# A hybrid block on one core: the memory's second value unit moves from the banded attention to the first norm

## The chip, the cores and the metric

The kernel runs on one core of a Trainium2 chip. The metric is the device time of one execution in microseconds (us), lower is better. The core has five engines with queues of their own that meet only at semaphores: TensorE (PE) for matmuls, VectorE (DVE), ScalarE (ACT), GpSimd (POOL) and SyncE (SP), which only issues DMAs here.

## What is computed

Two blocks in a row over 256 tokens of width 1024, in float32. The change lies in the first block:

```python
def first_block(x, mem, ...):
    h = hybrid_mixer(x, w_in, ...)            # mLSTM and banded attention, then @ w_out
    x = layer_norm(ALPHA * x + h, ln1_g, ln1_b)
    h = memory_cross_attention(x, mem, xa_wq, xa_wkv, xa_wo)
    x = layer_norm(ALPHA * x + h, ln2_g, ln2_b)
    ...

def memory_cross_attention(x, mem, wq, wkv, wo):
    q = (x @ wq).reshape(B, S, XA_HEADS, XA_HEAD_DIM)
    k, v = jnp.split(mem @ wkv, 2, axis=-1)
    ...
```

`mem` is an input of 256 rows of width 1024 and doesn't depend on `x`. So `mem @ wkv`, 1024 columns of keys and 1024 of values, can be multiplied at any time before the cross attention reads it.

## The kernel before

**Products.** A float32 product is made of three matmuls of rounded halves (`three`): high times high, low times high and high times low. Each operand has a high half in the rounded type and a low half, the rest. `hir` and `lor` hold the halves of the weights, `INH`/`INL` those of an activation, `HIH`/`HIL` those of another (here of `mem` in tiles 0 to 7 and of the mixer's output `mix` in tiles 8 to 15).

**Units and chunks.** A unit is 256 columns of a weight, in chunks of four 128-row tiles (48 matmuls of 256 columns), or, for values, a wide unit of 512 columns, in chunks of two tiles (48 matmuls of 512 columns, `wide_g`). The keys of the memory are the units kv 0 to 3, the values the wide units kv 4 and kv 5. The function `weight_plan` lists all chunks in order of use, and between them 48 rows "mod" of the modulation weights of the second block, which VectorE alone multiplies with a vector. A chunk costs a DMA of 512 KB into one of six raw buffers (SP waits until the chunk six places earlier has been split), an ACT instruction that rounds it (`hir<-raw`), and a DVE instruction that subtracts (`lor<-raw,hir`).

**Staging ahead.** The class `Ahead` decides where these two instructions stand in the queues of ACT and DVE. `take` is called where a unit's chunk comes due. It issues the split of that chunk if need be, then of the next ones until three are ahead. There are four slots for split chunks, so a chunk can be split only when the matmuls of the chunk four places earlier are done.

**The attention.** The mLSTM and the banded attention (`swa`, groups 0 and 1) are generators, and `rotate` interleaves their steps with those of a filler, `projections`, in the code of each engine. The filler runs through the first projections, then kv 0 to 5. A step of a wide unit's filler is one chunk, 12 matmuls. In `swa`, TensorE multiplies logits, ACT and DVE make probabilities, TensorE transposes these (12 per group), ACT copies the results out, and TensorE multiplies with the values (`ps<-FA` 128x512). DVE copies both groups' output, and ACT and DVE split it into tiles 4 to 7 of `mix`. What is left of the filler runs after the last product, ahead of the output projection, units wout 0 to 3.

**The first norm.** Behind each wout unit, DVE adds it to `X` and ACT squares `X`. The norm sums over features with one-column matmuls (`row_sums`: what is early, then the last part of `X`, then its squares), DVE and ACT make the mean and the factor of each token, TensorE broadcasts both over the partitions (`spread_bank`), and DVE subtracts and multiplies tile by tile (UNITS: one tile, one, then pairs). ACT scales them to `INH`, and for the pairs a second time to `X`, and DVE subtracts the low half `INL`. Then the query units xq 0 and xq 1 run interleaved over the eight tiles, with four chunks of weights, and xq 2 and xq 3 behind them.

Names: in the rows, L1595 and L1598 are helpers of DVE, L1096 the rounding of weights on ACT, L1226 and L1176 the copies of transposed probabilities and of values, L754 the transposes, L1259 and L1264 the two scalings of the norm.

Of the kernel before, what the change touches and what calls it, by code (L numbers as in the profile page):

```python
# [132 lines left out]
def weight_plan(A):  # L133

    plan = []
# [52 lines left out]
    for c in range(2):  # L188
        add_wide(("kv", 4 + c), A["xa_wkv"], 1024 + 512 * c, 8, mod=2)
    for c in range(4):  # L190
# [5 lines left out]
        add_mod(int(c < 3))  # L196
    add2(("xq", 0), A["xa_wq"], 0, ("xq", 1), A["xa_wq"], 256, mod=1)
# [124 lines left out]
def build(nc, A, out):  # L322
    with ExitStack() as ctx:
# [182 lines left out]
        def tensor(e):  # L506
# [58 lines left out]
            def wide_g(key, kt, x, pool=lin, apart=0):  # L565
# [19 lines left out]
                for kk in range(both):  # L585
                    for m in range(2):
                        step(kk, m)
                    if kk % 2 and kk + 1 < kt:
                        yield
# [60 lines left out]
            def projections():  # L650
# [14 lines left out]
                for c in range(2):  # L665
                    yield from wide_g(("kv", 4 + c), 8, mem)
                    yield
# [103 lines left out]
            def row_sums(name, c, src):  # L771
# [6 lines left out]
                t.then_inc(*mm.up((name, "early")))  # L778
                w.wait_ge(dve.at((name, "x", 3)))
                for m in range(2):  # L780
                    for i in range(2):
                        column(b[:, m:m + 1], src[:, i, :], m, o1024, last=i == 1)
                w.wait_ge(act.at((name, "sq", 3)))
# [10 lines left out]
            def layer_norm(name):  # L794
                row_sums(name, 3, X[:, 6:8, :])
                spread_bank((name, "mu"), SN[:, 0:2])
                spread_bank((name, "r"), SN[:, 6:8])
# [4 lines left out]
            layer_norm("n1")  # L802
# [273 lines left out]
        def scalar(e):  # L1076
# [72 lines left out]
            def projections():  # L1149
# [22 lines left out]
                for c in range(2):  # L1172
                    yield from ahead.unit_g(("kv", 4 + c), 8, 2)
                    for m in range(2):
                        w.wait_ge(mm.at(("unit", ("kv", 4 + c), m)))
                        e.activation(VC[:, m, 512 * c:512 * c + 512], bank["unit", ("kv", 4 + c), m], ACT.Copy).then_inc(  # L1176
                            *act.up(("out", ("unit", ("kv", 4 + c), m)), *(["KV"] if c and m else [])))
                    yield
# [71 lines left out]
            def layer_norm(name, gn, bn, inp, free):  # L1250
                if ahead.next < len(plan) and plan[ahead.next][3] is True and ahead.room():
# [3 lines left out]
                for k, n in UNITS:  # L1255
                    d = X[:, k:k + n, :]
# [1317 lines left out]
```

## Time and profile before

| | |
|---|---|
| median of 3 runs | 906.94 us (902.21, 906.94, 906.99) |
| the profiled execution | 907.06 us |
| its span on the core | 905.3 us |
| PE busy | 860.5 us, 95% |
| DVE busy | 651.4 us, 72% |
| ACT busy | 503.7 us, 56% |
| 16 DMA engines, queue of the weights | 57.0% |
| granted clock of TensorE, mean | 0.97 |

In the profile, times count from the start of the span, and a row of the timeline can stand for several instructions in a row (x12), with the idle time of the engine ahead of them and what ended it in brackets. A float32 matmul of attention or norm appears as more than one record. A matmul's duration runs over the next one's start, so the pitch between starts tells its cost. PEclk is the granted clock of TensorE: 1.00 is 2.4 GHz, 0.50 is 1.2 GHz.

### The profile page before, as it was taken

Reading aid. Unit: us, or ns where it says so; the run is one execution under the profiler, and the core shown is the slowest. Engines: PE = TensorE matmul, PEld = TensorE weight load, DVE = VectorE, ACT = ScalarE, POOL = GpSimd, SP = SyncE. Lnnn points to the kernel's source line nnn. Section 1 sums busy time; section 2 is a strip of 40 time slices with the busy share of each in tenths; the row PEclk is TensorE's granted clock in tenths of the full one; section 3 lists DMA queues with packets and bytes.
Section 4 is the critical chain, followed back from the end, with each engine's and each line's share of the span. In section 5 each row is a group of like instructions: output and inputs, shape, how many; then the busy total and the mean of one; then the engine's idle time right before and its main releaser. Section 6 shows DMA issues by size and latency. Waiting matters only on the chain.

```text
span 905.3 us, 15843 instructions
## 1 busy us (share of the span) xinstructions
PE 860.5 (95%) x6396; PEld 810.8 (90%) x6396; DVE 651.4 (72%) x1011; ACT 503.7 (56%) x723; POOL 7.6 (1%) x17
## 2 busy tenths in 40 slices
PE   8899997999899999999997999999899899999997
PEld 7789986889799999999997899898899899999886
DVE  5765787678567988887867896787798766665553
ACT  5643447455447666655455756777657554444342
POOL 0200000000000000000000000000000000000000
PEclk9999999989998999999998999999999799999999
DMA  9974556756062665667862376455575177775751
GB/s 339 244 216 138 171 182 195 215 172 229 28 185 72 214 186 185 187 196 240 261 210 70 118 251 185 147 187 181 169 233 166 60 250 225 233 233 186 168 204 47
DMA packets 139592, 166.89 MB, mean 184 GB/s; under 512 B 5520, under 2 KB 123280, under 8 KB 139520
## 3 DMA queue, kind: packets, MB, share of 16 engines
q1 hardware_dynamic: 137712, 162.82, 57.0%
q0 software_dynamic: 720, 2.02, 1.2%
q8 instruction: 50, 0.82, 0.4%
q10 hardware_dynamic: 1088, 1.05, 0.3%
q14 instruction: 22, 0.18, 0.1%
HBM read 164.62 MB, written 1.25 MB: 183 GB/s over the span
## 4 chain that ended last, share of the span: by engine, by line
PE 32%; DVE 12%; ACT 8%; issue 3%; DVEq 0%; ACTq 0%
PE ps L512 32%; DVE lor L1595 5%; DVE FA L1595 3%; ACT hir L1096 2%; DVE FA L1598 1%; ACT L1434 1%; DVE INL L1595 0%; ACT X L1366 0%; DVE raw L1612 0%; ACT HIH L1372 0%; ACT FA L1434 0%; DVE FA L2256 0%; DVE FA L1601 0%; ACT FA L1476 0%; DVE X L1595 0%
## 5 line engine op out<-in xcount | busy, mean ns | idle before, releaser
L1595 DVE TENSOR_TENSOR lor<-raw,hir 128x1024 fp32r<-128x1024 f32 (+1 forms) x267 | 309.9, 1178 | 118.8 <-ACT hir L1096 112.6
L1096 ACT ACTIVATE hir<-raw 128x1024 fp32r<-128x1024 f32 (+1 forms) x257 | 260.2, 1032 | 125.1 <-PE ps L512 105.3
L512 PE MATMUL ps<-INH,hir 128*128 128x256 f32 (+1 forms) x1064 | 306.9, 288 | 4.2 <-ACT INH L1259 2.5
L512 PE MATMUL ps<-INH,lor 128*128 128x256 f32 (+1 forms) x1064 | 302.4, 284 | 2.8 <-DVE lor L1595 2.7
L512 PE MATMUL ps<-INL,hir 128*128 128x256 f32 (+1 forms) x1064 | 303.0, 285 | 1.4 <-DVE INL L1595 1.2
L512 PEld LDWEIGHTS ps<-INH,hir 128*128 128x128 f32 x1064 | 204.9, 193 | 7.4 <-issue 6.1
L512 PEld LDWEIGHTS ps<-INH,lor 128*128 128x128 f32 x1064 | 204.5, 192 | 4.9 <-DVE lor L1595 3.9
L512 PEld LDWEIGHTS ps<-INL,hir 128*128 128x128 f32 x1064 | 204.0, 192 | 2.4 <-DVE INL L1595 2.4
L512 PE MATMUL ps<-HIH,lor 128*128 128x256 f32 x688 | 195.5, 284 | 5.2 <-DVE lor L1595 5.2
L512 PE MATMUL ps<-HIH,hir 128*128 128x256 f32 x688 | 197.9, 288 | 0.0
L512 PE MATMUL ps<-HIL,hir 128*128 128x256 f32 x688 | 194.0, 282 | 0.0
L512 PEld LDWEIGHTS ps<-HIH,lor 128*128 128x128 f32 x688 | 130.6, 190 | 7.5 <-DVE lor L1595 6.6
L512 PEld LDWEIGHTS ps<-HIH,hir 128*128 128x128 f32 x688 | 130.8, 190 | 4.1 <-issue 3.2
L512 PEld LDWEIGHTS ps<-HIL,hir 128*128 128x128 f32 x688 | 131.1, 191 | 0.0
L1598 DVE SCALAR_TENSOR_TENSOR FA<-ps,vec,FA 128x254 f32<-128x254 f32 (+2 forms) x130 | 53.2, 474 | 17.8 <-ACT FA L1106 17.8
L512 PE MATMUL ps<-hir,HIH 128*128 128x512 f32 (+1 forms) x136 | 54.0, 397 | 8.9 <-DVE HIL L1595 6.1
L1612 DVE SCALAR_TENSOR_TENSOR raw<-raw,cb 128x1024 f32<-128x1024 f32 x48 | 58.3, 1219 | 0.7 <-DMA raw<-in_mod_wT 0.7
L512 PE MATMUL ps<-lor,HIH 128*128 128x512 f32 (+1 forms) x136 | 53.0, 390 | 0.0
L512 PE MATMUL ps<-hir,HIL 128*128 128x512 f32 (+1 forms) x136 | 53.0, 390 | 0.0
L1106 ACT ACTIVATE FA<-ps,vec 128x256 f32<-128x256 f32 x58 | 29.4, 558 | 35.4 <-PE ps L512 35.4
L512 PE MATMUL ps<-FA 128*128 128x256 f32 (+6 forms) x212 | 39.8, 372 | 4.3 <-DVE FA L1595 3.5
L512 PEld LDWEIGHTS ps<-hir,HIH 128*128 128x128 f32 x136 | 27.1, 199 | 15.9 <-issue 10.3
(270 smaller groups left out, 793.6 us busy)
## 6 DMA issues: line engine op xcount, KB each, us to landing
raw<-in_w_in SPq DMA_DIRECT2D x64, 512.0 KB, 4.5
raw<-in_mod_wT SPq DMA_DIRECT2D x48, 512.0 KB, 4.5
raw<-in_ffn_w_up SPq DMA_DIRECT2D x44, 512.0 KB, 4.5
raw<-in_w_ffn_in SPq DMA_DIRECT2D x44, 512.0 KB, 4.8
raw<-in_w_ffn_out SPq DMA_DIRECT2D x22, 512.0 KB, 4.4
raw<-in_ffn_w_down SPq DMA_DIRECT2D x20, 512.0 KB, 5.0
raw<-in_xa_wkv SPq DMA_DIRECT2D x16, 512.0 KB, 3.8
raw<-in_xa_wq SPq DMA_DIRECT2D x8, 512.0 KB, 5.7
```

Of the source, the lines that this page charges most:

```text
L512: return e.matmul(o, l, r, start=start, stop=stop, skip_group_check=True)
L1096: e.activation(hi, src, ACT.Copy).then_inc(*w_hi.up(i))
L1106: e.activation(o[:, b, :], p[:, b * T:(b + 1) * T], ACT.Identity, scale=V(wname, (K - 1) * nb + i + b), bias=V(bname, i + b)).then_inc(*ac ...
L1434: e.activation(dst, wide2(bank["unit", ("gl", c)]), ACT.Sigmoid).then_inc(*act.up(("out", ("unit", ("gl", c)))))
L1595: return e.tensor_tensor(o, a, b, op)
L1598: return e.scalar_tensor_tensor(out=o, in0=a, scalar=s, in1=b, op0=op0, op1=op1)
L1612: e.scalar_tensor_tensor(out=v, in0=v, scalar=1.0, in1=CB[:, :], op0=MUL, op1=MUL, accum_out=MOD[:, key[1]:key[1] + 1]).then_inc(*dve.up(key))
```

## The change

The plan of weights lists kv 5 behind the wout units instead of behind kv 4, and its two mod rows now stand behind kv 4, four in all. `projections` ends with kv 4 on all three engines. TensorE multiplies kv 5 in steps of three matmuls (`fine`) between the steps of the first norm, and what is left, ahead of the queries, with banks of the attention's pool. In the norm's code of ACT and DVE, `next(other)` takes the chunks of kv 5, and so stages the queries' chunks. The copy of the values (`values(1)`) stands behind the norm.

```diff
 weight_plan:
-    for c in range(2):
-        add_wide(("kv", 4 + c), A["xa_wkv"], 1024 + 512 * c, 8, mod=2)
+    add_wide(("kv", 4), A["xa_wkv"], 1024, 8, mod=4)
...
+    add_wide(("kv", 5), A["xa_wkv"], 1536, 8)
     add2(("xq", 0), A["xa_wq"], 0, ("xq", 1), A["xa_wq"], 256, mod=1)
 tensor, wide_g:
-            def wide_g(key, kt, x, pool=lin, apart=0):
+            def wide_g(key, kt, x, pool=lin, apart=0, fine=False):
...
                     for m in range(2):
                         step(kk, m)
-                    if kk % 2 and kk + 1 < kt:
+                        if fine:
+                            yield
+                    if kk % 2 and kk + 1 < kt and not fine:
                         yield
 tensor, row_sums and layer_norm:
                 t.then_inc(*mm.up((name, "early")))
+                fill(2)
                 w.wait_ge(dve.at((name, "x", 3)))
...
+                fill(1)
                 w.wait_ge(act.at((name, "sq", 3)))
...
+                row_sums(name, 3, X[:, 6:8, :], fill)
+                fill(1)
                 spread_bank((name, "mu"), SN[:, 0:2])
+                fill(2)
                 spread_bank((name, "r"), SN[:, 6:8])
...
-            layer_norm("n1")
+            values = wide_g(("kv", 5), 8, mem, att, fine=True)
+            layer_norm("n1", lambda n: steps_of(values, n))
+            run(values)
 scalar (vector alike, without the values):
-            def layer_norm(name, gn, bn, inp, free):
-                if ahead.next < len(plan) and plan[ahead.next][3] is True and ahead.room():
+            def layer_norm(name, gn, bn, inp, free, other=None):
+                if other:
+                    next(other)
+                elif ahead.next < len(plan) and plan[ahead.next][3] is True and ahead.room():
                     ahead.stage()
...
                 for k, n in UNITS:
+                    if other and k in (0, 2, 4):
+                        next(other, None)
...
-            layer_norm("n1", "ln1_g", "ln1_b", x1, "x1 free")
+            layer_norm("n1", "ln1_g", "ln1_b", x1, "x1 free", ahead.unit_g(("kv", 5), 8, 2))
+            values(1)
```

**DVE at the end of the attention.** The rows from the last chunks of kv 4 to the probabilities of both groups (`small` holds their sums, `raw,cb` is a mod row). Before:

```order
L1595 TENSOR_TENSOR lor<-raw,hir 128x1024 x2
L1612 SCALAR_TENSOR_TENSOR raw,small<-raw,cb 128x1024 x2
L1595 TENSOR_TENSOR lor<-raw,hir 128x1024
L1595 TENSOR_TENSOR small<-small 128x8
L1796 RECIPROCAL small<-small 128x8
L1601 TENSOR_SCALAR FA<-FA,small 128x128 x4
```

After:

```order
L1609 TENSOR_TENSOR lor<-raw,hir 128x1024 x2
L1626 SCALAR_TENSOR_TENSOR raw,small<-raw,cb 128x1024 x4
L1609 TENSOR_TENSOR lor<-raw,hir 128x1024
L1609 TENSOR_TENSOR small<-small 128x8
L1809 RECIPROCAL small<-small 128x8
L1615 TENSOR_SCALAR FA<-FA,small 128x128 x4
```

Four mod rows now stand ahead of the first group's probabilities where two stood; the split behind them is that of a wout chunk.

**PE in the first norm.** From the sums of the last `X` (`con,X`) and its squares (`con,SQ`) to the broadcasts (`con,small`). Before, with the first query matmuls (`INH`) behind them:

```order
L512 MATMUL ps<-con,X 128x1 x4
L512 MATMUL ps<-con,SQ 128x1 x4
L512 MATMUL ps<-con,small 128x128 x4
L512 MATMUL ps<-INH,hir 128x256
L512 MATMUL ps<-INH,lor 128x256
L512 MATMUL ps<-INL,hir 128x256
```

After:

```order
L512 MATMUL ps<-con,X 128x1 x4
L512 MATMUL ps<-hir,HIH 128x512
L512 MATMUL ps<-hir,HIL 128x512
L512 MATMUL ps<-lor,HIH 128x512
L512 MATMUL ps<-con,SQ 128x1 x4
L512 MATMUL ps<-hir,HIH 128x512
L512 MATMUL ps<-hir,HIL 128x512
L512 MATMUL ps<-lor,HIH 128x512
L512 MATMUL ps<-con,small 128x128 x2
```

Three matmuls of kv 5 stand in each gap here, six ahead of the first row and six between the two broadcasts, and 30 behind the second, ahead of the queries.

**ACT in the first norm.** From the root (`small`) through the scalings to `INH` and `X` to the next roundings of weights (`hir`). Before:

```order
L1254 ACTIVATE small<-small 128x2
L1259 ACTIVATE INH<-X,vec 128x256 x4
L1264 ACTIVATE X<-X,vec 128x256 x2
L1259 ACTIVATE INH<-X,vec 128x256 x2
L1264 ACTIVATE X<-X,vec 128x256 x2
L1259 ACTIVATE INH<-X,vec 128x256 x2
L1264 ACTIVATE X<-X,vec 128x256 x2
L1096 ACTIVATE hir<-raw 128x1024 x7
```

After:

```order
L1265 ACTIVATE small<-small 128x2
L1103 ACTIVATE hir<-raw 128x1024
L1272 ACTIVATE INH<-X,vec 128x256 x2
L1103 ACTIVATE hir<-raw 128x1024
L1272 ACTIVATE INH<-X,vec 128x256 x2
L1277 ACTIVATE X<-X,vec 128x256 x2
L1103 ACTIVATE hir<-raw 128x1024
L1272 ACTIVATE INH<-X,vec 128x256 x2
L1277 ACTIVATE X<-X,vec 128x256 x2
L1272 ACTIVATE INH<-X,vec 128x256 x2
L1277 ACTIVATE X<-X,vec 128x256 x2
L1186 ACTIVATE FA<-ps 128x512 x2
```

The three roundings between the scalings are those of the first three query chunks; each is for a slot that kv 5 must free. The fourth comes behind the copies of the last row. DVE's splits stand in the same places.

## Rows read from the trace of the kernel before

**Rows 1.** the page: busy us of an engine (share of the span) xinstructions

```profile
PE 860.5 (95%) x6396; PEld 810.8 (90%) x6396; DVE 651.4 (72%) x1011; ACT 503.7 (56%) x723; POOL 7.6 (1%) x17
```

**Rows 2.** timeline, PE, end of the attention (start us, us, engine line op tiles)

```profile
150.08 2.47 PE L754 MATMUL ps<-con,FA 128*128 128x128 f32 x12 [2.59 <-DVE FA L1601]
...
152.20 0.78 PE L512 MATMUL ps<-hir,HIH 128*128 128x512 f32 x1
...
155.86 1.47 PE L754 MATMUL ps<-con,FA 128*128 128x128 f32 x12
157.08 0.48 PE L512 MATMUL ps<-hir,HIH 128*128 128x512 f32 x1
...
160.03 3.71 PE L512 MATMUL ps<-FA 128*64 128x512 f32 x12
163.67 0.49 PE L512 MATMUL ps<-hir,HIH 128*128 128x512 f32 x1
...
169.09 0.40 PE L512 MATMUL ps<-lor,HIH 128*128 128x512 f32 x1
```

**Rows 3.** timeline of DVE at the end of the attention

```profile
144.24 1.22 DVE L1612 SCALAR_TENSOR_TENSOR raw<-raw,cb 128x1024 f32<-128x1024 f32 x1
...
146.53 1.22 DVE L1595 TENSOR_TENSOR lor<-raw,hir 128x1024 fp32r<-128x1024 f32 x1
...
148.10 1.93 DVE L1601 TENSOR_SCALAR FA<-FA,small 128x128 f32<-128x128 f32 x8
...
151.51 1.93 DVE L1601 TENSOR_SCALAR FA<-FA,small 128x128 f32<-128x128 f32 x8
...
166.19 1.23 DVE L1595 TENSOR_TENSOR HIL<-FA,HIH 128x1024 fp32r<-128x1024 f32 x1 [1.13 <-ACT HIH L1101]
```

**Rows 4.** timeline of PE in and behind the first norm; the last: cross attention

```profile
193.50 1.05 PE L512 MATMUL ps<-con,X 128*128 128x1 f32 x8 [0.51 <-DVE X L1598]
...
196.11 2.25 PE L512 MATMUL ps<-con,small 128*128 128x128 f32 x8 [0.25 <-DVE small L1853]
199.60 0.55 PE L512 MATMUL ps<-INH,hir 128*128 128x256 f32 x1 [1.24 <-ACT INH L1259]
...
205.22 0.28 PE L512 MATMUL ps<-INH,hir 128*128 128x256 f32 x1
...
211.94 0.28 PE L512 MATMUL ps<-INH,hir 128*128 128x256 f32 x1
...
229.83 0.66 PE L825 MATMUL ps<-con,FA 128*128 128x128 f32 x4 [1.17 <-DVE FA L1601]
```

**Rows 5.** three stretches of PE: length, busy us (x), PEclk, DMA share, GB/s

```profile
150.00:153.80 3.80, 3.72 (x16) 0.56 0.78 282
153.80:160.00 6.20, 6.20 (x34) 0.99 0.84 249
196.00:205.00 9.00, 7.57 (x31) 0.50 0.03 10
```

**Rows 6.** timeline of ACT at the end of the attention

```profile
144.94 2.94 ACT L1096 ACTIVATE hir<-raw 128x1024 fp32r<-128x1024 f32 x3
147.79 1.06 ACT L1176 ACTIVATE FA<-ps 128x512 f32<-128x512 f32 x2
```

**Rows 7.** timeline of SP's queue, end of the attention: weight requests

```profile
140.90 3.87 SPq L2443 DMA_DIRECT2D raw<-in_xa_wkv  x2
```

**Rows 8.** timeline of DVE in the first norm

```profile
195.89 0.16 DVE L1853 COPY small<-ps 128x4 f32<-128x4 f32 x1 [2.45 <-PE ps L512]
...
198.40 1.21 DVE L1595 TENSOR_TENSOR X<-X,ps 128x256 f32<-128x256 f32 x3 [0.61 <-PE ps L512]
...
204.68 1.22 DVE L1595 TENSOR_TENSOR lor<-raw,hir 128x1024 fp32r<-128x1024 f32 x1
205.81 1.40 DVE L1595 TENSOR_TENSOR X<-X,ps 128x512 f32<-128x512 f32 x2
```

**Rows 9.** timeline of ACT in the first norm

```profile
202.88 1.09 ACT L1264 ACTIVATE X<-X,vec 128x256 f32<-128x256 f32 x2
```

More of the change, by code:

```diff
@@ L664, in projections @@
                     yield
-                for c in range(2):
-                    yield from wide_g(("kv", 4 + c), 8, mem)
-                    yield
+                yield from wide_g(("kv", 4), 8, mem)
+                yield
             b, before = att.get("uf", bank)
@@ L769, in tensor, with row_sums @@
             run(fill)
-            def row_sums(name, c, src):
+            def row_sums(name, c, src, fill=lambda n: None):
                 b, before = att.get((name, "sums"), bank)
@@ L792, in spread_bank, with layer_norm @@
                 spread(b, v, name)
-            def layer_norm(name):
-                row_sums(name, 3, X[:, 6:8, :])
+            def layer_norm(name, fill=lambda n: None):
+                row_sums(name, 3, X[:, 6:8, :], fill)
+                fill(1)
                 spread_bank((name, "mu"), SN[:, 0:2])
+                fill(2)
                 spread_bank((name, "r"), SN[:, 6:8])
@@ L1171, in projections, with values @@
                     yield
[L1172 to L1178, printed above, removed]
+                yield from ahead.unit_g(("kv", 4), 8, 2)
+                values(0)
+                yield
+            def values(c):
+                for m in range(2):
+                    w.wait_ge(mm.at(("unit", ("kv", 4 + c), m)))
+                    e.activation(VC[:, m, 512 * c:512 * c + 512], bank["unit", ("kv", 4 + c), m], ACT.Copy).then_inc(
+                        *act.up(("out", ("unit", ("kv", 4 + c), m)), *(["KV"] if c and m else [])))
             w.wait_ge(mm.at("uf f"), dve.at("UC"))
@@ L1712, in projections @@
                     yield
-                for c in range(2):
-                    yield from ahead.unit_g(("kv", 4 + c), 8, 2)
-                    yield
+                yield from ahead.unit_g(("kv", 4), 8, 2)
+                yield
             w.wait_ge(mm.at("uf f"))
@@ L1846, in stats, with layer_norm @@
                     fold(st, (name, "m", 2), (name, "sum"))
-            def layer_norm(name, gn, bn, inp, free):
+            def layer_norm(name, gn, bn, inp, free, other=None):
                 low = None
-                if ahead.next < len(plan) and plan[ahead.next][3] is True and ahead.room():
+                if other:
+                    next(other)
+                elif ahead.next < len(plan) and plan[ahead.next][3] is True and ahead.room():
                     low = ahead.enter()
@@ L1877, in layer_norm @@
                 for k, n in UNITS:
+                    if other and k in (0, 2, 4):
+                        next(other, None)
                     d = X[:, k:k + n, :]
@@ L1893, in vector @@
                 stats("n1", c, None)
-            layer_norm("n1", "ln1_g", "ln1_b", x1, "x1 free")
+            layer_norm("n1", "ln1_g", "ln1_b", x1, "x1 free", ahead.unit_g(("kv", 5), 8, 2))
             dve.mark("before cross attention")
```

## The prediction, made before the changed kernel ran

> **What bounds the kernel now.** I read the page first: the tensor engine is busy 95% of the span [rows 1]. So a matmul that moves is paid at its new place unless it fills a gap there, and leaves its old place only if the engine has nothing else to wait for. Then I read two stretches in the timelines: the end of the banded attention, from 143 us to the start of the output projection (wout) at 169.3 us, and the first norm, from 192.04 us, the end of wout, to the end of the two interleaved query units.
>
> In the attention the matmuls of the second value unit (key kv 5, called V5 here; 48 wide ones) stand in three pieces: 12 at 152.20 behind the first transposes, 12 at 157.08 behind the second, and 24 from 163.67, behind the last product of probabilities and values [rows 2]. The last piece covers a chain on two other engines: the two attention outputs are copied, rounded and subtracted, until 167.42 [rows 3]. In the norm the engine does little: one-column sums and four broadcasts until 198.36, then it waits until 199.60 for the first normalized tile [rows 4]. That makes some 7.6 us of room for V5, which is 48 x 0.236 = 11.3 us long (the pitch from the first to the last of the 24: 163.67 to 169.09 [rows 2]).
>
> **Part 1: taken out of the attention.** What then ends last is the vector engine. Its next vector multiplies for the modulation (mod) are four in a row now, because the value weights between them are gone: two more at 1.15 us (144.24 to 146.53 for two), ahead of the first probabilities, which began at 148.10. They now end at about 152.3, the second ones (begun at 151.51, 1.9 us long) at 155.7 [rows 3]. Both sets slip by 2.3 us. The transposes of the first follow at 152.4. The engine has then idled for 4.9 us; after 2.6 us of idling the first of the old ones ran at 1.2 GHz (0.56 granted until 153.8), taking 2.1 us where the second, at the full clock, took 1.2 [rows 2, 5]. The second transposes start at 155.8 and, still at 1.2 GHz, end at 157.9; the scalar engine copies the last bank (two such copies took 1.06 us [rows 6]), and the product starts at 158.4. It took 3.64 us at 2.4 GHz (160.03 to 163.67 [rows 2]), and would take 7.3 at half of it. The full clock came back at 153.8, 3.7 us after work resumed [rows 2, 5]; counted from 155.8 that is 159.5 to, allowing for the 5.6 us of the norm (199.60 to 205.22 [rows 4, 5]), 161.4. I take 160.5, so the product ends at 163.0; bounds 162.0 (clock back at once) and 165.5 (never during the product).
>
> The scalar engine is the other guard of that time: it rounds three chunks in a row at 144.94 before its copies [rows 6]. They are now wout chunks. The first takes the place of the first request of the row of 140.90 [rows 7], which had landed by 146.9, when its rounding, the third of those, began. The third is requested at 146.7, when the second mod is done; with the same 5 to 6 us it is rounded by 153, ahead of the first copy. A later landing would push the product out by as much.
>
> Now the cover is gone. Wout begins at 163.0, does 24 matmuls (2.83 us) and then wants the attention's output, low half too, 3.75 us after the product's end (163.67 to 167.42 [rows 2, 3]). It waits 0.7 us. Wout ends at 163.0 + 3.75 + 2.6 + 17.0 = 186.4 instead of 192.04. **Gain 5.6 us**, bounds 3.1 and 6.6. So only half of V5 is won back: its last piece hid a chain, and its first two stood where the vector engine is late anyway.
>
> **Part 2: put into the norm.** I count from the end of wout. On the tensor engine: early sums 0.9 (the eight records of the X sums took 0.9, 193.50, the next ones 0.91 later [rows 4]; the early ones are eight too), 6 matmuls of V5 1.4, the sums of the last X 0.9, 3 matmuls 0.7, the sums of its squares 1.0 (an estimate from the same eight records), at +5.0; 3 matmuls to +5.7; broadcast of the mean, 6 matmuls to +7.6, broadcast of the factor to +8.2 (0.66 with its tail for four records at the full clock, so some 0.5 each [rows 4]). Then 30 matmuls in a row until +15.1. If only this counted, the queries' 96 matmuls at 0.118 (205.22 to 211.94 for 57 [rows 4]) would end at +26.5. Before they ended at 213.7, +21.7. That is a cost of 4.9.
>
> But the weights count too. Before, three of the four first query chunks lay ready ahead of the norm and the fourth was split beside it (204.68 [rows 8]). Now the four slots hold V5, and each query chunk can be rounded only when V5's matmuls have freed a slot, by a scalar and a vector instruction that stand between the norm's steps. The scalar queue: root to +6.0, first chunk to +7.0 (1.0 each [rows 6]). The vector engine waits for that, splits until +8.2 (1.22 [rows 8]), subtracts, and its next multiplication starts at +8.6 instead of at 198.40, +6.4. Pair by pair:
> the second chunk is rounded at +10.3 behind the first two scalings and split until +12.5; tiles 2 and 3 are normalized by +13.8 (1.40 for a pair less the overlap [rows 8]); the scalar engine scales them twice, 1.1 each [rows 9], until +16.0, and only then rounds the third chunk, split at +18.2. Tiles 4 and 5 are normalized at +19.6; the low half of tiles 2 and 3 follows at +20.2. On the scalar engine tiles 4 and 5 last until +21.8 and tiles 6 and 7 until +23.9; then V5's two results are copied (1.05 [rows 6]), and the fourth chunk is rounded until +26.0 and split until +27.2. Nothing covers this last split: it stands behind the whole norm.
>
> The tensor engine follows: V5 ends at +15.1, tiles 0 and 1 are multiplied until +18.0, it waits for the low half of tile 2 until +20.2, works until +23.6, and waits for the fourth chunk until +27.2. The remaining 41 matmuls end at +32.0. **Cost 10.3 us** instead of 4.9. The last wait is 3.6 us long; one of 2.6 us was followed by 1.2 GHz and cost about 1.8 us (transposes 0.9 too long, the 12 wide ones 3.66 instead of 2.8, which is 12 x 0.236 [rows 2, 5]). **Cost 1.8 us**, bounds 0 and 2.3 (24 matmuls at the pitch that they had before 205.22 [rows 4]).
>
> Whether the short pieces in the norm run at 2.4 GHz is not shown in the old norm, which lay at 0.50 from 196 to 205 with one-column work [rows 5]. With 2 matmuls out of 3 us dense between them I take the full clock. The Trainium skill (Perfetto Trace Analysis, Matmul Optimizations) says that power follows utilization and that matmuls should run back to back in batches. That speaks against pieces of 3 and 6; by it the sum would be the third case below, by my reading the first.
>
> Behind the queries nothing changes: the chunks for the third and fourth units are split before the tensor engine gets there (at most four instructions of 1.2 us in the 7 us it still computes), the attention's values are copied 7 us before they are read, and the later stages are bound by the tensor engine, which gives nothing back. The weights' bytes are the same.
>
> **Sum.** -5.6 + 10.3 + 1.8 = **+6.5 us**. The profiled execution took 907.06 us, the median of the runs shown is 906.94; so **913.5 us**. With all bounds: -6.6 + 10.3 + 0 = +3.7 to -3.1 + 10.3 + 2.3 = +9.5.
>
> **Rivals.** First, *the room is real*: the splits don't hold the norm. If the fourth query chunk is split by +21.7, when the tensor engine would want it, and the low halves keep ahead of it, only the 4.9 us remain: -5.6 + 4.9 = -0.7, 906.4 us, and down to 905.3 with the best clock in the attention. For it: the vector engine idled 2.45 us for the sums before [rows 8], and the engine that is 95% busy had a hole there. Against it: the order above, in which the scalar engine reaches the fourth rounding only after the last scaling. The Trainium skill (Perfetto Trace Analysis, Optimization Strategy) recommends interleaving regimes bound by different engines; by it this case would hold. It decides at 5.5 us: by so much must the scalar and vector chain be shorter than my sum. No sum of mine reaches 4.5 us faster.
>
> Second, *the pieces run at 1.2 GHz*. The first gap closes late, V5's pieces cost 0.42 each and free the slots later: 3 + 3 + 6 matmuls at 0.19 more each are 2.3 us, the sums and broadcasts about 1.0 more. The chain above shifts by 3.3 and all behind it: +9.8, 916.9 us.
>
> Third, *the wout weights land late*: the scalar engine waits for the third chunk, two us beyond 153, and the attention ends with it: +8.5, 915.5 us. Against it: the queue is asked for the same bytes per time as before.
>
> **How the numbers follow.** Forecast 0.60; the room is real 0.22; half clock 0.08; late weights 0.05; something faster that I have no price for 0.05. A measurement can tell 0.5%, 4.5 us. Of the forecast's 0.60 some 0.08 falls below 4.5. Slower: 0.52 + 0.13 = 0.65; same: 0.22 + 0.08 = 0.30; faster 0.05. The range takes in the first rival, whose chance is over what may be left out, and the second: 905.0 to 918.0.
>
> **What would show it.** The product of probabilities and values ending near 163, wout's end near 186.4, a wait of about 0.7 us in its first unit. In the norm the vector engine should wait for the scalar engine's roundings (three times), the tensor engine for a low half of tile 2 (2.2 us) and for the fourth query chunk (3.6 us), and the query units should end about 32 us after wout instead of 21.7. If V5 ran into the queries without waits, the first rival holds; if wout ends at 189 or later, part 1 is too hopeful.

## The result, and the profile after

| | before | after |
|---|---|---|
| median | 906.94 us (902.21 to 911.43, 9 runs) | 911.28 us (909.66 to 914.91, 9 runs) |
| the profiled execution | 907.06 us | 912.93 us |
| its span | 905.3 us | 911.1 us |

The ratio after to before is 1.0067, with a 95% interval of 1.0046 to 1.0088: the change costs 6.1 us (4.2 to 8.0) by that ratio. The medians alone differ by 4.3 us, the profiled executions by 5.9 us.

The page of after hides this completely: TensorE does the same work, in nearly the same busy time as in [rows 1].

```profile
PE 859.0 (94%) x6396; PEld 809.2 (89%) x6396; DVE 651.7 (72%) x1011; ACT 503.6 (55%) x723; POOL 7.6 (1%) x17
```

**Where the time went.** ScalarE loads a function table 43 times, always at the same places of the program. Three of these loads bracket the two changed stretches: at the attention's probabilities, at the third wout unit, and at the start of the cross attention. These are the rows of ScalarE's timeline (start us, duration), before and then after:

```profile
128.15 1.28 ACT L1218 ACT_TABLE_LOAD   x1
...
187.93 1.28 ACT L1111 ACT_TABLE_LOAD   x1
...
223.55 1.28 ACT L1284 ACT_TABLE_LOAD   x1
```

```profile
128.28 1.28 ACT L1227 ACT_TABLE_LOAD   x1
...
182.77 1.28 ACT L1118 ACT_TABLE_LOAD   x1
...
229.28 1.28 ACT L1298 ACT_TABLE_LOAD   x1
```

From the first to the second, the attention stage, went from 59.78 to 54.49 us: 5.3 gained. From the second to the third, the norm stage (it has the rest of wout in it, 4.1 us in both), from 35.62 to 46.51 us: 10.9 lost. Every later load comes 5.7 to 5.9 us later than before, up to the last. So in these two executions the whole difference lies in the two stages, and nothing behind them gives back or adds. All experiments below are read with the same two numbers.

**The attention after**, PE's timeline (idle time ahead and what ended it in brackets), against [rows 2]:

```profile
152.50 2.50 PE L755 MATMUL ps<-con,FA 128*128 128x128 f32 x12 [4.88 <-DVE FA L1615]
...
156.93 2.82 PE L755 MATMUL ps<-con,FA 128*128 128x128 f32 x12 [1.92 <-ACT FA L1235]
...
159.68 3.70 PE L512 MATMUL ps<-FA 128*64 128x512 f32 x12
...
167.12 0.38 PE L512 MATMUL ps<-HIL,hir 128*128 128x256 f32 x1 [0.47 <-DVE HIL L1609]
```

With no value matmuls between them, the transposes wait 4.88 us for the four mods, as forecast. The second transposes wait 1.92 us more, and not for VectorE but for ScalarE's copy of the first ones. ScalarE was late since it had stood at a DMA:

```profile
150.15 1.06 ACT L1103 ACTIVATE hir<-raw 128x1024 fp32r<-128x1024 f32 x1 [4.03 <-DMA raw<-in_w_out]
154.36 1.06 ACT L1103 ACTIVATE hir<-raw 128x1024 fp32r<-128x1024 f32 x1 [3.15 <-DMA raw<-in_w_out]
155.32 1.07 ACT L1186 ACTIVATE FA<-ps 128x512 f32<-128x512 f32 x2
```

The third wout chunk is rounded until 155.4, not 153. SP's queue sent its request on time, at 146.77, but it landed 7.6 us later and not 5 to 6. Two rows, SP's timeline and the weights' requests of 138 to 158 us (size, median us to landing):

```profile
146.77 2.41 SPq L2460 DMA_DIRECT2D raw<-in_w_out  x3
```

```profile
raw<-in_w_out SPq DMA_DIRECT2D x3, 512.0 KB, 7.6
```

The clock, in stretches (length, busy us of PE, PEld, DVE, ACT, POOL, then PEclk, DMA share, GB/s):

```profile
149.00:152.00 3.00, 0.00 (x0) 0.00 (x0) 2.93 (x12) 1.06 (x1) 0.00 (x0) 1.00 0.94 296
152.00:154.00 2.00, 1.50 (x9) 1.50 (x10) 1.93 (x6) 0.00 (x0) 0.00 (x0) 0.72 1.14 229
154.00:158.00 4.00, 2.08 (x10) 1.68 (x9) 4.00 (x11) 3.50 (x6) 0.00 (x0) 0.50 1.05 291
158.00:160.00 2.00, 2.00 (x10) 1.54 (x9) 0.13 (x1) 1.41 (x3) 0.00 (x0) 0.57 1.15 202
160.00:163.00 3.00, 3.00 (x12) 0.99 (x10) 0.00 (x0) 0.38 (x1) 0.00 (x0) 1.00 1.03 245
```

The low clock begins within the first transposes (0.72 from 152 to 154), covers the second, and ends ahead of the product of probabilities and values, which took 3.6 us as before. This early end is particular to this execution: in the six others with the same code up to wout (e1, e2, e3, e9, e10, e11 below) the low clock reached into the product, which took 3.9 to 4.3 us.

**The norm after**, PE, against [rows 4]:

```profile
189.15 0.95 PE L512 MATMUL ps<-con,X 128*128 128x1 f32 x8
...
194.16 0.61 PE L512 MATMUL ps<-con,small 128*128 128x128 f32 x4
...
207.47 0.58 PE L512 MATMUL ps<-INL,hir 128*128 128x256 f32 x1 [2.69 <-DVE INL L1609]
...
213.14 0.38 PE L512 MATMUL ps<-INH,hir 128*128 128x256 f32 x1 [0.57 <-ACT hir L1103]
214.50 0.38 PE L512 MATMUL ps<-INH,lor 128*128 128x256 f32 x1 [0.98 <-DVE lor L1609]
```

and the two engines that it waits for, ScalarE and then VectorE, against [rows 9] and [rows 8]:

```profile
200.96 1.09 ACT L1272 ACTIVATE INH<-X,vec 128x256 fp32r<-128x256 f32 x2 [2.71 <-DVE X L1609]
202.09 1.10 ACT L1277 ACTIVATE X<-X,vec 128x256 f32<-128x256 f32 x2
203.09 1.05 ACT L1103 ACTIVATE hir<-raw 128x1024 fp32r<-128x1024 f32 x1
206.85 1.09 ACT L1272 ACTIVATE INH<-X,vec 128x256 fp32r<-128x256 f32 x2 [2.71 <-DVE X L1609]
...
211.08 1.06 ACT L1186 ACTIVATE FA<-ps 128x512 f32<-128x512 f32 x2
212.04 2.94 ACT L1103 ACTIVATE hir<-raw 128x1024 fp32r<-128x1024 f32 x3
```

```profile
198.38 1.23 DVE L1609 TENSOR_TENSOR lor<-raw,hir 128x1024 fp32r<-128x1024 f32 x1 [0.93 <-ACT hir L1103]
...
204.26 1.23 DVE L1609 TENSOR_TENSOR lor<-raw,hir 128x1024 fp32r<-128x1024 f32 x1 [2.56 <-ACT hir L1103]
205.41 1.40 DVE L1609 TENSOR_TENSOR X<-X,ps 128x512 f32<-128x512 f32 x2
206.73 0.68 DVE L1609 TENSOR_TENSOR INL<-X,INH 128x512 fp32r<-128x512 f32 x1
...
213.22 1.23 DVE L1609 TENSOR_TENSOR lor<-raw,hir 128x1024 fp32r<-128x1024 f32 x1 [1.25 <-ACT hir L1103]
```

The reader sees two engines taking turns: VectorE waits 2.56 us for a rounding, ScalarE waits 2.71 us for the tiles that VectorE normalizes behind the split of that rounding, and TensorE waits for what comes out, three times. V5's pieces themselves ran at the full clock (the idle time in the first row is the start of the wait that ends at 207.47), the low one came behind the first wait:

```profile
186.00:206.00 20.00, 18.78 (x115) 16.50 (x113) 12.80 (x23) 8.19 (x13) 0.00 (x0) 1.00 0.41 132
208.00:210.80 2.80, 2.80 (x15) 2.80 (x14) 1.39 (x3) 2.77 (x6) 0.00 (x0) 0.50 0.15 53
```

### The profile page after: what moved, and what is told of

It is laid out like the page before. It is cut to its first block, busy times and chain, and to the rows that moved or that the text cites. A ratio compares the mean times of both kernels' runs of the same rounds, so it can differ in the third digit from the quotient of the medians.

```text
span 911.1 us, 15842 instructions
## 1 busy us (share of the span) xinstructions
PE 859.0 (94%) x6396; PEld 809.2 (89%) x6396; DVE 651.7 (72%) x1011; ACT 503.6 (55%) x723; POOL 7.6 (1%) x17
## 3 DMA queue, kind: packets, MB, share of 16 engines
HBM read 164.62 MB, written 1.25 MB: 182 GB/s over the span
## 4 chain that ended last, share of the span: by engine, by line
PE 30%; DVE 13%; ACT 8%; issue 3%; DMA 1%; DVEq 0%; ACTq 0%; SPq 0%
PE ps L512 30%; DVE lor L1609 5%; DVE FA L1609 3%; ACT hir L1103 2%; DVE FA L1612 1%; ACT L1448 1%; DMA raw<-in_ffn_w_down 1%; DVE INL L1609 0%; ACT X L1380 0%; DVE raw L1626 0%; ACT HIH L1386 0%; ACT FA L1448 0%; DVE FA L2273 0%; DVE FA L1615 0%; ACT FA L1490 0%
## 5 line engine op out<-in xcount | busy, mean ns | idle before, releaser
L1609 DVE TENSOR_TENSOR HIL<-FA,HIH 128x512 fp32r<-128x512 f32 (+2 forms) x34 | 23.4, 690 | 23.6 <-ACT HIH L1108 23.0
```

Source lines behind the costliest of these rows:

```text
L1609: return e.tensor_tensor(o, a, b, op)
```

## The experiments

The theory after the result: the attention is held by VectorE's mods, and the norm by a chain of roundings and splits of query chunks on ScalarE and VectorE, not by TensorE's work. The rivals: TensorE's time for V5 costs what it costs, wherever it stands; or each wait has a cause of its own.

The eleven kernels of the experiments in one table, with before and after. The stages are measured in one profiled execution of each, as above; "sum" is both, against before. A ratio is the estimate of the kernel's time over that of the kernel before, from all runs of both on the same chip, with its 95% interval. The medians come from several chips, on which the kernel before had 906.94 (after), 905.54 (e1 to e4), 904.96 (e5b to e8b) and 906.08 us (e9 to e11), so kernels are compared by their ratios.

| kernel | attention stage | norm stage | sum | median | ratio |
|---|---|---|---|---|---|
| before | 59.78 | 35.62 | 0 | | 1 |
| after | 54.49 | 46.51 | +5.6 | 911.28 | 1.0067 (1.0046 to 1.0088) |
| e1 early rounding | 54.18 | 39.96 | -1.3 | 905.61 | 1.0005 (0.9992 to 1.0017) |
| e2 a third of V5 | 54.03 | 45.88 | +4.5 | 911.14 | 1.0056 (1.0028 to 1.0083) |
| e3 V5 as one block | 55.41 | 45.33 | +5.3 | 908.01 | 1.0028 (1.0007 to 1.0050) |
| e4 no mods | 50.63 | 48.06 | +3.3 | 911.21 | 1.0054 (1.0032 to 1.0075) |
| e5b e1, no mods | 50.68 | 39.96 | -4.8 | 902.37 | 0.9959 (0.9933 to 0.9985) |
| e6b e1, two mods | 49.95 | 39.97 | -5.5 | 901.06 | 0.9949 (0.9928 to 0.9971) |
| e7b e1, mods at keys | 51.83 | 39.97 | -3.6 | 905.73 | 1.0009 (0.9990 to 1.0027) |
| e8b before, no mods | 59.40 | 35.61 | -0.4 | 904.34 | 0.9999 (0.9975 to 1.0023) |
| e9 copies later | 54.54 | 45.56 | +4.7 | 909.21 | 1.0051 (1.0028 to 1.0073) |
| e10 third chunk early | 54.51 | 45.26 | +4.4 | 909.31 | 1.0042 (1.0019 to 1.0065) |
| e11 both of these | 54.23 | 44.49 | +3.3 | 908.28 | 1.0057 (1.0032 to 1.0083) |

Behind the norm the executions differ by up to 3 us from one to the next at two or three places (around 454 to 530 us and at 640 us), and some reach 128 us 2 us later than others, in kernels that differ only later. So the stage numbers are sharper than the medians, the norm's above all: the four kernels with e1's norm agree to 0.01 us, and so do before and e8b. The attention stage is less sharp. Seven kernels have the same code up to wout (after, e1, e2, e3, e9, e10, e11) and took 54.0 to 55.4 us. And an execution that reaches 128 us 2 us late (e2, e4, e5b, e9, e10) makes up 1.0 us of it ahead of the first transposes: these start 23.3 us behind the first load in e2, e9 and e10, and 24.2 us behind it in after, e1, e3 and e11. Differences of less than some 1.5 us in the whole of that stage show nothing; its part up to the first transposes repeats to 0.02 us among executions that are alike at 128 us.

**e1: the splits don't stand between the norm's steps.** ScalarE rounds a chunk as soon as its slot can be free, and the fourth ahead of tiles 4 to 7; VectorE likewise.

```diff
 scalar, layer_norm:
-                    if other and k in (0, 2, 4):
+                    if other and k in (0, 2):
                         next(other, None)
+                    if other and k == 2:
+                        next(other, None)
+                    if other and k == 4:
+                        ahead.stage()
 vector, layer_norm: at the loop's head nothing; behind the tail of the pair before:
+                    if other and k in (1, 2, 4):
+                        next(other, None)
+                    if other and k == 6:
+                        ahead.stage()
```

> The changed kernel, with the same matmuls, but ScalarE rounds the third query chunk ahead of the scalings of tiles 2 and 3 and the fourth ahead of those of tiles 4 and 5, and VectorE's four splits stand behind the low halves of each step instead of ahead of the normalizing ones. Theory (the splits of the query chunks hold the norm, ScalarE's order above all): the query units end 26 to 27 us behind wout instead of 32.4, the two waits of 2.7 and 1.5 us go, and the time falls by 5 to 6 us against the changed kernel, to 905 to 908 us, about that of the kernel before. Rival (TensorE's time in the norm is what was added, 11.3 us of matmuls, wherever the splits stand): no change, 911 us.

The norm stage fell by 6.6 us, to 39.96, and the queries end 26.0 us behind wout instead of 32.5 (21.7 before). No wait of TensorE is left from wout's end to the third query unit; in one stretch:

```profile
186.00:220.00 34.00, 34.00 (x246) 31.92 (x245) 28.73 (x45) 20.23 (x29) 0.00 (x0) 1.00 0.62 192
```

TensorE is busy without a gap, and at the full clock. The instructions are the same as in after; only their order on two engines differs. So it is shown that the order of the splits is the cause of 6.6 of the 10.9 us lost in the norm; the other 4.3 are what V5's matmuls cost there. As a whole e1 is no faster than before: its ratio is 1.0005.

**e2: 16 of V5's 48 matmuls**, high times high alone; the two low products are left out.

```diff
 tensor, wide_g (kv 5 alone):
-                        t = three(b, x.hi[:, kk, tk], x.lo[:, kk, tk], hi[:, k, :], lo[:, k, :], kk == 0, kk == kt - 1)
+                        t = mul(b, x.hi[:, kk, tk], hi[:, k, :], start=kk == 0, stop=kk == kt - 1)
```

> The changed kernel with only high times high for the second value unit: 16 of its 48 matmuls, 3.8 us instead of 11.3; the splits stay. The two low products of these values are left out. Theory: the chain of splits and scalings ends last, so the 7.5 us of matmuls that are gone give back only what frees the slots and the sums earlier, about 2 us: 909 us. Rival: TensorE's time counts in full, 7.5 us less: 904 us.

32 matmuls fewer, 7.6 us of TensorE's work, gave 0.6 us in the norm stage, not even the 2 us of the theory. TensorE now waits 5.9 us for splits and low halves, where it waited 4.2 us in after, and the last of these waits ends 27.0 us behind wout, where it ended at 27.6:

```profile
200.44 0.39 PE L512 MATMUL ps<-INH,lor 128*128 128x256 f32 x1 [0.98 <-DVE lor L1612]
...
202.54 0.40 PE L512 MATMUL ps<-INL,hir 128*128 128x256 f32 x1 [1.01 <-DVE INL L1612]
...
208.23 0.58 PE L512 MATMUL ps<-INL,hir 128*128 128x256 f32 x1 [2.95 <-DVE INL L1612]
...
215.25 0.38 PE L512 MATMUL ps<-INH,lor 128*128 128x256 f32 x1 [0.97 <-DVE lor L1612]
```

So the rival that TensorE's work is the price falls, from the other side than in e1.

**e3: V5 in one block between wout and the norm**, on all three engines.

```diff
-            values = wide_g(("kv", 5), 8, mem, att, fine=True)
-            layer_norm("n1", lambda n: steps_of(values, n))
-            run(values)
+            run(wide_g(("kv", 5), 8, mem, att))
+            layer_norm("n1")
```

> The changed kernel, but the second value unit runs as one block between the output projection and the norm, and the norm is that of the kernel before (query chunks staged ahead of it). TensorE pays 11.3 us in full, the norm and the queries take the old 21.7 us. Theory: the stretch from the end of wout to the end of the queries is 33 us against 32.4 in the changed kernel, so filling the norm gained nothing: 911 to 913 us. Rival (the norm's room was used at least for some us): 914 to 918 us.

The norm stage took 45.33 us, 9.7 more than before, and 1.2 less than with the pieces between the steps. V5 is paid nearly in full here: its block takes 11.1 us, and the norm and the queries behind it 1.4 us less than before (20.3 us for 21.7). And yet this is no worse than the change. All that the change hid beside the norm, its chain took back. The expectation had 0.6 us more than in after where it was 1.2 less, and 911 to 913 us where the median is 908.01; the ratios of e3 and after (1.0028 and 1.0067) differ by more than the 0.3 us of the two stages, and the rest has no explanation here.

**e4: none of the four mods ahead of the probabilities.** They stand behind units of the cross attention's output instead.

```diff
 weight_plan:
-    add_wide(("kv", 4), A["xa_wkv"], 1024, 8, mod=4)
+    add_wide(("kv", 4), A["xa_wkv"], 1024, 8, mod=0)
...
-        add(("xo", c), A["xa_wo"], 256 * c, 8)
+        add(("xo", c), A["xa_wo"], 256 * c, 8, mod=1)
```

> The changed kernel with its four modulation rows behind the first value unit moved into the four units of the cross attention's output projection (xo). Theory for the attention (what ends last there is VectorE with four rows of 1.15 us ahead of the probabilities, and behind it ScalarE, which waits for the DMA of wout chunks that are asked for late): both go, the product with the values ends 4 to 6.6 us earlier than 163.3, wout ends by as much earlier, and xo has room on VectorE: 905 to 907 us. Rival (a wait elsewhere takes its place, in wout or xo where VectorE gets more to do): 909 to 911 us.

The attention stage gained 3.9 us over after (e5b gained 3.5 over e1), of which 1.0 us each is the late start described above. But the norm stage lost 1.5 of it. TensorE's waits there are the same as in after (2.67, 0.58 and 0.97); this time the clock fell behind the last of them (212.91) as well:

```profile
213.00:217.00 4.00, 4.00 (x21) 4.00 (x22) 4.00 (x5) 0.39 (x1) 0.00 (x0) 0.57 0.74 180
```

where after, behind its own last wait at 214.50, had this:

```profile
215.00:219.00 4.00, 4.00 (x37) 4.00 (x36) 4.00 (x7) 0.01 (x1) 0.00 (x0) 1.00 0.69 220
```

21 matmuls in 4 us against 37. Another 1.0 us went where the mods now stand, and 3.0 us more around 500 us, where executions differ anyway; so the median shows nothing of the gain, and the time is that of the rival.

**e5b, e6b, e7b: e1 with the mods elsewhere.** In e5b all four behind feed-forward units 4 to 7, in e6b two of them, in e7b all four behind the key units.

```diff
 e5b:
-    add_wide(("kv", 4), A["xa_wkv"], 1024, 8, mod=4)
+    add_wide(("kv", 4), A["xa_wkv"], 1024, 8, mod=0)
-        add(("up", 11 + c), A["ffn_w_up"], 2816 + 256 * c, 8)
+        add(("up", 11 + c), A["ffn_w_up"], 2816 + 256 * c, 8, mod=int(4 <= c < 8))
 e6b: mod=2 behind kv 4, int(4 <= c < 6) behind up
 e7b: mod=0 behind kv 4, and
-        add(("kv", c), A["xa_wkv"], 256 * c, 8, mod=1)
+        add(("kv", c), A["xa_wkv"], 256 * c, 8, mod=2)
```

> The kernel with the early rounding, and in addition none of the four mod multiplies stands in the attention: they stand behind the feed-forward's units 4 to 7, one each. Theory (two separate chains, one in the attention and one in the norm, each with its own price): the attention gives what it gave when the four mods were taken out alone, wout's end about 3.9 us earlier than in the early-rounding kernel (near 182.7), the norm runs without waits of the tensor engine, and the cross attention starts about 5.0 us earlier than in the kernel before (1.1 + 3.9); 900.5 to 902. Rival (something gives the time back, as when the mods went out alone: a low clock behind the norm's last wait, or a chain of the scalar engine that was hidden so far): the cross attention starts at most 2 us earlier than before, 904 to 906.

> The kernel with the early rounding, with two mod multiplies ahead of the probabilities, as many as before, and the other two behind the feed-forward's units 4 and 5. Theory (2.3 us of the vector engine ahead of the first transposes are what the change lost in the attention): the transposes start near 150.1 as before instead of 152.5, wout ends 1.9 to 2.4 us earlier than in the early-rounding kernel, cross attention 3.0 to 3.5 us earlier than before; about 902 to 903. Rival (the attention's end is set by the roundings of wout chunks on the scalar engine, whose weights land late): wout's end moves by less than 1 us.

> The kernel with the early rounding, and the four mod multiplies of the attention's end one each behind the key units kv 0 to 3, where one stands already. Theory: same gain at the attention's end as with them in the feed-forward (3.9 us), less what the vector engine loses at 100 to 140 us, where it is 77% busy and the tensor engine 95%: between 0 and 2.3 us; the cross attention starts 3 to 5 us earlier than in the kernel before. Rival (the vector engine bounds the mLSTM at this place, so that four multiplies more are paid in full): 4.6 us lost ahead of 143 us, and the time as with the early rounding alone, near 905.5.

The norm stage is the same in e1, e5b, e6b and e7b (39.96, 39.96, 39.97, 39.97): with the early rounding, what the attention gains stays. Against before, the two stages give e5b 4.8 us, where the theory had 5.0, and e6b 5.5, where it had 3.0 to 3.5. By the ratios e6b is 0.5% faster than before and 1.2% faster than after, and e5b 0.4% faster than before. Taking out two mods gave 4.2 us over e1, more than the 1.9 to 2.4 of the theory, and in the profiles taking out the other two as well gave it up again in part. In time the two can't be told apart: their intervals overlap (0.9928 to 0.9971, 0.9933 to 0.9985). PE in e6b:

```profile
150.38 2.82 PE L755 MATMUL ps<-con,FA 128*128 128x128 f32 x12 [2.59 <-DVE FA L1619]
153.88 1.50 PE L755 MATMUL ps<-con,FA 128*128 128x128 f32 x12 [0.68 <-ACT FA L1235]
155.31 3.71 PE L512 MATMUL ps<-FA 128*64 128x512 f32 x12
```

and in e5b:

```profile
150.76 1.84 PE L755 MATMUL ps<-con,FA 128*128 128x128 f32 x12 [2.19 <-DVE FA L1619]
154.26 2.79 PE L755 MATMUL ps<-con,FA 128*128 128x128 f32 x12 [1.66 <-DVE FA L1619]
156.98 4.52 PE L512 MATMUL ps<-FA 128*64 128x512 f32 x12
```

Against after, e6b's first transposes come 2.1 us earlier (152.50 to 150.38), as the theory said. The request for the third wout chunk leaves 2.1 us earlier too (144.69 for 146.77) and lands sooner, so that ScalarE has rounded it by 149.1 and the second transposes wait only 0.68 us for its copies, not 1.92. In e1 they hardly waited either (0.68 us); against e1 the rest of the gain is the clock: the second transposes took 1.50 instead of 2.79 us, the product 3.71 instead of 4.33. Why the clock came back earlier, no run shows.

With no mod left (e5b) the first transposes come only 0.4 us sooner than with two, once the late start is taken off, as in e8b below: VectorE then waits for ScalarE's third rounding. And the low clock falls later, behind a full clock on the first transposes, and lasts into the product (4.52 us):

```profile
150.00:152.00 2.00, 1.24 (x11) 1.24 (x12) 1.97 (x6) 0.55 (x2) 0.00 (x0) 0.96 0.65 220
152.00:154.00 2.00, 0.60 (x3) 0.20 (x1) 1.97 (x9) 1.14 (x3) 0.00 (x0) 0.50 0.22 67
```

e4, with the same attention, had the same: 0.53 from 152 to 154 and a product of 4.47 us. e7b lost 4.0 us against e1 ahead of 128 us and came out as e1 did in the median, as its rival said; up to 2 us of these may be the difference between executions named above, so how much the key units charge for the four mods stays open between 2 and 4 us.

**e8b: before, without its four mods there.**

> The kernel before the change with its four mod multiplies of the attention's end (two of them ahead of the first probabilities) moved behind the feed-forward's units 4 to 7. Theory: the first transposes start 2.3 us earlier, the tensor engine's wait of 2.59 us ahead of them all but goes, and with it the low clock of 150 to 153.8 (0.9 us): wout ends 2.5 to 3.5 us earlier than in the kernel before, 903.4 to 904.5. So moving the value unit away would be worth 1.5 to 3 us of its own (this against the early rounding without mods). Rival (the tensor engine has value matmuls to do in that time anyway and the third piece covers the rest): less than 1 us at wout's end, 906 to 907.

The attention stage gained 0.4 us: the rival's case, though for another reason than it gave. With the mods gone, VectorE waits for ScalarE's third rounding in a row:

```profile
145.83 1.23 DVE L1595 TENSOR_TENSOR lor<-raw,hir 128x1024 fp32r<-128x1024 f32 x1 [1.79 <-ACT hir L1096]
```

so that the probabilities come 0.7 us earlier (147.40 for 148.10 in [rows 3]), not 2.3, and 0.3 of these were there at 128 us already. Moving the mods is worth nothing that the ratio shows (0.9999) without moving V5, and neither is moving V5 with the early rounding alone (1.0005 in e1); the two together give 3.7 us (e5b) and 4.6 us (e6b).

**e9, e10, e11: which split costs what.** On after: the two copies of V5's results behind the roundings of the query chunks (e9), the third chunk's rounding on ScalarE ahead of the scalings of tiles 2 and 3 (e10), both (e11).

```diff
 e9, scalar:
-            values(1)
             act.mark("before cross attention")
             ahead.units([("xq", 0), ("xq", 1)], 8)
+            values(1)
 e10, scalar, layer_norm:
-                    if other and k in (0, 2, 4):
+                    if other and k in (0, 2):
                         next(other, None)
+                    if other and k == 2:
+                        next(other, None)
```

> The changed kernel, with the scalar engine's two copies of the moved value unit's results behind the roundings of the first query chunks instead of ahead of the fourth one (212.04 in the changed kernel). Theory (a chain of the scalar and vector engines holds the norm, and it ends with the fourth query chunk): the fourth rounding starts 2.0 us earlier, the tensor engine's last two waits (0.57 and 0.98) go, the first one (2.69) stays, and the queries end 1.55 us earlier than in the changed kernel; about 909.7. Rival (the copies lie beside waits anyway): less than 0.5 us.

> The changed kernel, with the scalar engine's rounding of the third query chunk (203.09 in the changed kernel) ahead of the scalings of tiles 2 and 3 instead of behind them; the vector engine's order is as in the changed kernel. Theory (chain): the third chunk is split when the vector engine gets there, 2.5 us earlier, tiles 4 to 7 and with them the fourth rounding come 2.5 us earlier; the tensor engine's first wait (2.69) all but goes, but it then stands earlier at the fourth chunk and waits longer for it, so that the queries end only 2.5 us earlier than in the changed kernel; about 908.8. Rival (each wait of the tensor engine has its own price): the 2.69 us and the low clock behind it (1.4 us) go in full, 4.1 us. Second rival (all work of the scalar engine counts, whatever its order): 0 us.

> Both edits together on the changed kernel: the third chunk's rounding early, and the two copies behind the query chunks' roundings. Theory (chain): 2.5 + 2.0 = 4.5 us, as far as the tensor engine's own work allows, that is at most the 6.5 us that the early rounding of all chunks gave; cross attention 4.5 us earlier than in the changed kernel, about 906.7. Rival (prices of the waits): 4.1 + 1.55 = 5.6 us, 905.6.

They gave 0.95, 1.25 and 2.0 us in the norm stage. In e9 the two copies turned out to take 1.0 us together (211.08 to 212.04 in after), not the 2.0 expected: the fourth chunk's rounding starts 0.95 us earlier, and TensorE gets just that. The wait for its high half (0.57) is gone, that for its low half stays (0.86). In e10 and e11 the chain moved by 2.6 and 3.6 us, and TensorE got less. In e10 the fourth chunk's rounding comes 2.6 us earlier (it starts 26.63 us after the stage's table load instead of 29.27), and the first wait of 2.69 is gone. TensorE then stands at the fourth chunk:

```profile
212.72 0.39 PE L512 MATMUL ps<-INH,hir 128*128 128x256 f32 x1 [2.11 <-ACT hir L1103]
214.08 0.58 PE L512 MATMUL ps<-INH,lor 128*128 128x256 f32 x1 [0.97 <-DVE lor L1611]
```

and the low clock, which in after fell into a stretch that waited anyway, follows here behind the last wait: 0.50 from 214 to 216. That takes back 1.4 of the 2.6 us. In e11 the last wait ended 3.6 us earlier than in after, and 1.6 of these went the same way (0.50 from 212 to 215). So neither the plain chain as expected (2.0, 2.5 and 4.5) nor the price of each wait (4.1 and 5.6) gave the sizes. The chain as measured (0.95, 2.6 and 3.6) less the low clock behind its last wait (0, 1.4 and 1.6) does, an account made after these runs; and only e1, which leaves no wait, gets the 6.6 us.

## Why the prediction was right, and where it was not

The time came out at 912.93 for the profiled execution and 911.28 in the median, where 913.5 was forecast; slower, as given the highest chance. The chain that was to hold the norm was the right one; the nearness of the total is in part luck, since a term of 1.8 us fell away and two others came out 0.4 and 0.6 us dearer. By its steps:

- **The bound** and the shape of the answer held: V5 left a place where TensorE waited for others, and came to one where others had no time left.
- **Gain of the attention, 5.6 us:** 5.2 to 5.3 measured. Wout ended at 186.88 (186.4). Two of its terms were off, and nearly cancelled by luck. The third wout chunk was to be rounded by 153, and was at 155.4, which pushed the second transposes from 155.8 to 156.93 and the product from 158.4 to 159.68. That is the third rival's condition in full (2 us beyond 153), at a price of 1.3 us instead of 2. The landing of 5 to 6 us was too short: from request to rounding it took 6.1 to 8.3 us in the seven executions with this code, 7.6 in the middle one. The clock was to come back at 160.5, in the middle of the product, and came back ahead of it, so the product took 3.6 instead of 4.6 us; in the six other executions it came back within the product, as forecast, which took 3.9 to 4.3 us. The wait in wout was 0.5 us (0.7).
- **Cost of the norm, 10.3 us:** 10.9 measured. The chain came out step by step: the low half of tile 2 at +20.6 (+20.2), the fourth chunk at +27.6 (+27.2), both counted from wout's end. What was left out is 0.4 us ahead of the first of them, and 0.1 behind the last. V5 itself ended at +14.7 (+15.1; from the terms given it would have been +15.3).
- **The wait for the fourth chunk, 3.6 us:** 1.6 us in two pieces (0.57 at its high half, 0.98 at its low half). TensorE came later than said, since the low clock behind the first wait lay in this stretch.
- **Clock behind the last wait, 1.8 us:** 0 in the profile of after. This is the term that failed in the execution on record. The low clock came behind the first wait, from 208 to 210.8, where 14 matmuls at 0.213 instead of 0.118 cost 1.3 us that the chain hid. e4, e10 and e11 had it behind the last one, at 1.4 to 1.6 us: the size was fair, the place was not certain.
- **The sum:** -5.3 + 10.9 + 0 = +5.6 against +6.5.
- **A reading of the old norm:** the prediction put its 0.50 from 196 to 205 us down to one-column work. The one-column sums stood ahead of it, from 192 to 196 us, at 1.00 and then 0.72; the low stretch has the broadcasts, the wait of 1.24 us and the first query matmuls.
- **The Trainium skill** (Perfetto Trace Analysis, Matmul Optimizations) on matmuls in back-to-back batches: the pieces of 3 and 6 ran at 1.00 from 186 to 206 us, with TensorE busy without a gap until the wait ahead of 207.47, so the second rival fell. Its advice to interleave regimes bound by different engines (same page, Optimization Strategy) is what e1 shows at work, with a condition that this case adds: only when nothing that the filler needs stands in line between the other's steps.
- **The first rival, the room is real**, fell as the change was written, and is true of the room itself. With the splits out of the way (e1), V5 costs 4.3 us in the norm stage (39.96 against 35.62), where the rival said 4.9 for its 11.3 us of work.

Two claims stay without a test: why some executions reach 128 us 2 us later than others, and what decides when the clock falls and how long it stays low behind waits of much the same length.

## What to carry to other kernels

When work moves into a gap of one engine, list what it needs on the others, and where these instructions stand in their queues. Here 11.3 us of matmuls fitted for 4.3, but four roundings and splits between the norm's steps made two engines take turns, and cost 6.6 us more. Look at what the emptied place exposes as well: the mods, which had cost 0.4 us beside V5 (e8b), had to move with it, and only both together beat the kernel before.

## What the runs showed of the hardware

- How waits and the low clock hang together is less plain than the prediction had it. Waits of 2.69, 0.57 and 0.98 us in after left the clock at 1.00 behind the last; nearly the same waits in e4 were followed by 0.57 over 4 us. At the attention's end e6b waited 2.59 and 0.68 us and had the full clock for the second transposes and the product (3.71 us); e1 waited 4.89 and 0.68 and had the low one until 160 us (4.33 us). After and e3 waited 4.88 and 1.92, 4.88 and 2.10 us; their products took 3.70 and 4.13. In e5b the first transposes, behind a wait of 2.19 us, ran at 0.96, and the clock was at 0.50 from 152 to 158 us, before and behind a second wait of 1.66.
- The low clock that fell ahead of a wait for others in after (208 to 210.8 us, 1.3 us of longer matmuls) cost nothing. In e10 and e11, with the first wait removed, one fell behind the last wait, and 1.4 and 1.6 us were paid.
- Pieces of three wide matmuls among one-column sums and broadcasts kept TensorE at 2.4 GHz for 20 us (PEclk 1.00 from 186 to 206), where before, without them, the clock was at 1.00 for the first sums (192 to 194), 0.72 for the rest (194 to 196), and 1.2 GHz from the broadcasts on (0.50 from 196 to 205 in [rows 5]).
- The same 512 KB requests, in the same order and in after and e1 at the same times to 0.1 us, landed in 7.6 us in one execution and in 6.0 in the other (138 to 158 us); over the seven executions with this code the medians were 6.0 to 8.3.
